# Moving the copies of a rarely entered overflow loop to VectorE, and a wait out of its If, in a hybrid decoder layer

## What is computed

```python
def hier_moe(x2d, ...):                   # 544 rows, top-1 of 4 groups, top-2 of its 8 experts
    ...                                   # e_glob: two experts for each row; w_top: their weights
    order = jnp.argsort(e_flat)
    ...                                   # rows sorted by expert, padded to blocks of 64
    def run_block(args):
        toks, e = args
        xb = x2d[toks]
        hb = jax.nn.silu(xb @ w_g[e]) * (xb @ w_u[e])
        return hb @ w_d[e]
    ...                                   # weighted outputs added back to each row
```

## Time and profile before

| | |
|---|---|
| median of 3 runs | 1580.1 us |
| lowest and highest run | 1578.76 and 1707.49 us |
| the profiled execution, its own time | 1580.1 us |
| the profiled execution, its span from the first to the last instruction | 1578.4 us |
| busy: PE / PEld / DVE / ACT / POOL | 1362.0 / 811.7 / 390.8 / 353.0 / 87.3 us |
| mean granted TensorE clock | 0.919 |

### The profile page before, as it was taken

One profiled execution on the slowest core, in us unless ns is written; L12 is line 12 of the kernel. 1 busy time (PEld: TensorE's weight loads), 2 busy tenths in 40 slices (PEclk: granted clock), 3 DMA queues, 4 the chain that ended last, 5 costly groups with the idle time before them and its releaser, 6 DMA issues.

```text
span 1578.4 us, 22203 instructions
## 1 busy us (share of the span) xinstructions
PE 1362.0 (86%) x8780; PEld 811.7 (51%) x8780; DVE 390.8 (25%) x691; ACT 353.0 (22%) x566; POOL 87.3 (6%) x144
## 2 busy tenths in 40 slices
PE   7999988986999999887699997978988888788873
PEld 5847444464676767554578884553333333233321
DVE  2013333333444444442010012241101010101113
ACT  2122233232544544664000001110100000000000
POOL 3000000002000000200000000010111001100100
PEclk9999999997999999999799998978998898889987
DMA  6113200005999999999680116036999999999984
GB/s 217 54 56 121 80 0 0 0 0 153 327 372 343 361 370 313 386 385 368 224 308 24 54 54 221 27 147 260 428 425 426 426 426 427 425 426 426 423 369 180
DMA packets 119640, 395.94 MB, mean 251 GB/s; under 512 B 17075, under 2 KB 25284, under 8 KB 107250
## 3 DMA queue, kind: packets, MB, share of 16 engines
q1 hardware_dynamic: 109506, 380.41, 62.1%
q0 software_dynamic: 5984, 11.18, 2.0%
q10 hardware_dynamic: 4048, 2.93, 0.6%
HBM read 386.06 MB, written 16.27 MB: 255 GB/s over the span
## 4 chain that ended last, share of the span: by engine, by line
PE 73%; issue 7%; DVE 6%; DMA 5%; SPq 4%; ACT 4%; ACTq 1%; POOLq 0%; DVEq 0%
PE ps L1091 16%; PE ps L932 8%; PE ps L1114 7%; PE ps L629 7%; PE ps L755 6%; PE ps L632 4%; PE ps L935 4%; PE ps L990 3%; PE ps L766 3%; DMA arena<-in_cache_k 3%; SPq L356 2%; PE ps L788 2%; PE ps L684 2%; SPq L348 1%; PE ps L688 1%
## 5 line engine op out<-in xcount | busy, mean ns | idle before, releaser
L1091 PE MATMUL ps<-arena 128*64 128x512 f32 x512 | 260.1, 667 | 73.5 <-issue 72.0
L1092 PE MATMUL ps<-arena 128*64 128x512 f32 x512 | 260.5, 669 | 0.0
L1091 PEld LDWEIGHTS ps<-arena 128*64 128x64 f32 x512 | 75.7, 154 | 222.5 <-issue 220.3
L755 PE MATMUL ps<-ident,arena 128*128 128x128 f32 x1024 | 149.3, 292 | 25.8 <-DMA arena<-in_cache_k 20.0
L755 PEld LDWEIGHTS ps<-ident,arena 128*128 128x128 f32 x1024 | 117.8, 148 | 96.2 <-issue 67.8
L1308 ACT ACTIVATE arena<-ps 128x512 f32<-128x512 f32 x192 | 108.7, 595 | 170.2 <-PE ps L755 170.0
L629 PE MATMUL ps<-mixers,arena 128*128 128x272 f32 x512 | 121.2, 399 | 0.5 <-DVE mixers L1460 0.5
L932 PE MATMUL ps<-mixers,arena 128*128 128x272 f32 x512 | 120.1, 396 | 0.0
L629 PEld LDWEIGHTS ps<-mixers,arena 128*128 128x128 f32 x512 | 98.5, 193 | 21.2 <-DVE mixers L1460 0.6
L932 PEld LDWEIGHTS ps<-mixers,arena 128*128 128x128 f32 x512 | 98.3, 192 | 20.5 <-issue 0.4
L632 PE MATMUL ps<-arena,mixers 128*128 128x512 f32 (+1 forms) x240 | 105.4, 595 | 0.0
(11 more groups left out here) (319 smaller groups left out, 1376.3 us busy)
## 6 DMA issues: line engine op xcount, KB each, us to landing
arena<-in_cache_k SPq DMA_DIRECT2D x256, 256.0 KB, 5.1
arena<-in_cache_v SPq DMA_DIRECT2D x256, 256.0 KB, 5.0
arena<-in_w_gate_exp SPq DMA_DIRECT2D x32, 2048.0 KB, 27.8
arena<-in_w_up_exp SPq DMA_DIRECT2D x32, 2048.0 KB, 32.2
arena<-in_w_down_exp SPq DMA_DIRECT2D x22, 2048.0 KB, 23.6
mixers<-in_w_down_exp SPq DMA_DIRECT2D x10, 2048.0 KB, 23.2
arena<-in_w_in SPq DMA_DIRECT2D x7, 2048.0 KB, 8.9
arena<-in_w_in SPq DMA_DIRECT2D x8, 1024.0 KB, 8.3
```

The source lines that it names most:

```text
L755: last = turn(ps[:, TURN + j % 2, P * c:P * c + P], kring[n % 3][:, j, P * c:P * c + P], ident[:, :])
L1091: mm(ps[0:BLK, 1 + u, :], own, wgv[w][:, k, :], start=k == 0, stop=k == KD - 1)
L1092: last = mm(ps[BLK:P, 1 + u, :], own, wuv[w][:, k, :], start=k == 0, stop=k == KD - 1)
```

## The change

- SP: the wait for `down` to reach 32 moves from the first place in the body of the If to a place ahead of the reading of the count, so ahead of the whole loop.
- POOL, in the body: the multiplication of gate and up is gone, and its waits are renumbered.
- ScalarE, in the body: the eight scaled copies of turned rows, the copy of the up product and the copy of the turned hidden values are gone. The SiLU and the output copy stay.
- VectorE: gets a loop of its own over the 17 passes, between `hidden_cols(31)` and the wait for the first read of `expert_outs`, with a wait for the table and a reading of the count ahead of it. In its body it scales the turned rows in one instruction, multiplies gate and up with the up product read from PSUM, and copies the turned hidden values.
- TensorE, in the body: waits for VectorE's semaphore in place of ScalarE's and POOL's.

```diff
             sp.wait_ge(S("extra_table"), 1)
+            sp.wait_ge(S("down"), NE)
             novf = sp.value_load(tab[0:1, NOVF:NOVF + 1], min_val=0, max_val=NOVF)
             with sp.Fori(0, NOVF) as i:
                 e = sp.value_load(tab[0:1, bass.ds(i, 1)], min_val=0, max_val=NE - 1)
                 with sp.If(i < novf):
-                    sp.wait_ge(S("down"), NE)
                     sp.wait_ge(S("extra_products"), extra_stage(i, 0))
...
-                    pool.wait_ge(S("extra_act"), 5 * i + 3)
-                    pool.sem_inc(S("pool_passed"), 1)
-                    nc.gpsimd.tensor_tensor(m_s[0][0:BLK, :], m_s[0][0:BLK, :], m_s[1][0:BLK, :], ALU.mult
-                                            ).then_inc(S("extra_pool"), 1)
-                    pool.wait_ge(S("extra_act"), 5 * i + 5)
+                    pool.wait_ge(S("extra_act"), 2 * i + 2)
...
-                    pe.wait_ge(S("extra_act"), 5 * i + 1)
+                    pe.wait_ge(S("extra_dve"), 3 * i + 1)
...
-                    pe.wait_ge(S("extra_pool"), i + 1)
+                    pe.wait_ge(S("extra_dve"), 3 * i + 2)
...
-                    pe.wait_ge(S("extra_act"), 5 * i + 4)
+                    pe.wait_ge(S("extra_dve"), 3 * i + 3)
...
                 with act.If(i < novf):
-                    act.wait_ge(S("extra_products"), extra_stage(i, 1))
-                    for k in range(KD):
-                        last = fn(xgT[0][:, k, 0:BLK], ps[:, 3 + k // 4, P * (k % 4):P * (k % 4) + BLK], ACT.Copy,
-                                  scale=w2c[:, k:k + 1])
-                    last.then_inc(S("extra_act"), 1)
                     act.wait_ge(S("extra_products"), extra_stage(i, 2))
                     fn(m_s[0][0:BLK, :], ps[0:BLK, 1, :], ACT.Silu).then_inc(S("extra_act"), 1)
-                    fn(m_s[1][0:BLK, :], ps[0:BLK, 2, :], ACT.Copy).then_inc(S("extra_act"), 1)
-                    act.wait_ge(S("extra_products"), extra_stage(i, 3))
-                    fn(flat(m_h[:, 0]), ps[:, 7, 0:FJ * BLK], ACT.Copy).then_inc(S("extra_act"), 1)
...
                 hidden(n)
                 hidden_cols(n)
+            dve.wait_ge(S("extra_table"), 1)
+            novf = dve.value_load(tab[0:1, NOVF:NOVF + 1], min_val=0, max_val=NOVF)
+            with dve.Fori(0, NOVF) as i:
+                with dve.If(i < novf):
+                    dve.wait_ge(S("extra_products"), extra_stage(i, 1))
+                    got = ps[:, 3:5, :].rearrange("p b (k m) -> p (b k) m", k=4)[:, :, 0:BLK]
+                    v.tensor_tensor(xgT[0][:, :, 0:BLK], got, w2c.unsqueeze(2).to_broadcast([P, KD, BLK]), ALU.mult
+                                    ).then_inc(S("extra_dve"), 1)
+                    dve.wait_ge(S("extra_act"), 2 * i + 1)
+                    own = m_s[0][0:BLK, :]
+                    v.tensor_tensor(own, own, ps[0:BLK, 2, :], ALU.mult).then_inc(S("extra_dve"), 1)
+                    dve.wait_ge(S("extra_products"), extra_stage(i, 3))
+                    v.tensor_copy(flat(m_h[:, 0]), ps[:, 7, 0:FJ * BLK]).then_inc(S("extra_dve"), 1)
+                with dve.Else():
+                    dve.nop()
+                dve.nop()
+
             for i, r in enumerate(ROWS):
                 dve.wait_ge(S(f"y_loaded_{i}"), 16)
```

## The result

The changed kernel takes 1597.53 us in the median (1594.39 to 1600.62, four runs), the kernel before 1579.43 in the same comparison. The ratio is 1.011, with a 95% interval of 1.0088 to 1.0133: 1.1% slower, under the 2% that the forecast called hard to tell from no change, but clear of zero. The one run of 1707.49 us of the kernel before is 8% slower than its other runs and doesn't enter the ratio. The forecast was 1595.0, in a range of 1591 to 1600. The profiled execution took 1598.59 us, its span is 1596.8.

What follows compares the result with a forecast made beforehand. The prediction took the tail's chain from the last down product through SP's reads of expert_outs as what matters. Body edits 0, VectorE's loop 0 and SP's wait +14.9 us on 1580.1 gave 1595.0 us, range 1591 to 1600.

Steps and rivals of the forecast that it cites:

- The edits in the body cost nothing: Body of the If on ScalarE, POOL, VectorE, TensorE: no pass enters it, so removed and added cost are 0.
- rival D: Loop over extra blocks: the count is not zero in the measured runs; given no chance of its own.
- VectorE's loop is hidden: VectorE's new loop, 10.8 us, ends before the first read of expert_outs lands, so it adds 0.
- The cover: VectorE's wait for the first read of expert_outs, hiding its loop; at least 8.7 us remain at SP's pass.
- SP's shift: SP's first issue of the expert_outs reads moves from 1557.68 to 1572.6, +14.9 us.
- SP's wait puts the loop on the chain: SP's count read and 17 empty passes now follow the last down product: +14.9 us; chance 0.80.
- Rival A: SP's 17 passes cost more or less after the last product: 1591.8 to 1598.9 us; chance 0.12.
- Rival B: VectorE's loop becomes the bound, each pass waiting for a short transfer: 1610.4 us, with two 1642.7; chance 0.05.
- Rival C: SP's moved loop is hidden anyway at L455, under 3.9 us or behind a late scatter: 1580 us; chance 0.01.
- The own range of the forecast: Whole kernel: 1593 to 1597 us around 1595.0, from undisturbed runs 1.3 us apart.
- the wide range: Whole kernel: 1591 to 1600 us, taking in both ends of SP's other pass prices with that scatter.
- everything up to 1553 unchanged: Stretch ahead of the last product's end: the profile should show no shift there, else the prediction is wrong.

Runs made afterwards that it cites:

- the two-loop kernel: All of the change but SP's moved wait, plus a second loop of 17 empty passes behind VectorE's first; ratio to the kernel before 0.9999 to 1.0047.

## Why the prediction was right, point by point

**The edits in the body cost nothing.** Right for this input. VectorE's queue has 17 branches at its If and no instruction of the body, so the count is zero here too (rival D), and the kernel with all of the change but the wait shows no difference. What the edits do to an extra block that has rows, no run here shows.

**VectorE's loop is hidden.** Right, and its size was nearly so: 10.8 us forecast; from the count's read at 1552.6 to the last branch at 1562.6 it is 10.0, with a pass of (1562.3 - 1553.7) / 16 = 0.54 us against the 0.58 taken from ScalarE. The loop's start was taken 0.4 us too late, at the end of the last column copy; the count's read stands at the copy's start. The cover was 8.7 us of spare time at SP's pass and 17.2 at the pass taken, and 18.5 were measured. The statement that without SP's shift one loop at ScalarE's pass would still cost nothing holds too: it is the kernel with all but the wait.

**SP's wait puts the loop on the chain.** Right, and the term was well sized. From release to first issue 19.0 us was forecast (1553.6 to 1572.6) and 19.3 measured in three traces; the shift is 15.2 us against 14.9. Of the 0.3 more, 0.2 are one read of the table, 0.486 us where the other sixteen take 0.26 to 0.28; without it the passes are 1.08 apart as before, and the rest is under 0.1. The long read is no accident of one execution: it is the third pass's, 3.04 us after the last copy starts, in each of the four traces in which SP reads in its loop after the last product (0.486 to 0.496). No early loop has one as long (at most 0.333). It falls together with the transfers of the last scatter (about 1559.6 to 1560.4 in the changed kernel, the read from 1559.85 to 1560.34), but whether these, or the place in the loop, make it long was not tested.

**Rival A, passes of another price after the last product.** It had 0.12 and did not come: from release to first issue it is 0.3 us more than forecast, not 3.9 more nor 3.2 less. The price that the Trainium skill gives for a tensor_load (DMA: Bandwidth & Descriptors, latency and other measured facts), about 600 ns, isn't borne out on SP: the reads of its loop take 0.27 us in the median and 0.496 at most. Of its other reads in the kernel before, one of 128 took 0.699, with the median at 0.301.

**Rival B, a transfer waited for in each pass of VectorE's loop.** Did not come: 17 passes at 0.54 us, the next 17 of the two-loop kernel at 0.53. The page of the changed kernel counts the transfers of the queue that it calls instruction (number, MB, share), and the page of the kernel before has the same line:

```profile
q8 instruction: 71, 1.16, 0.3%
```

One of the 71 falls into the 10 us of VectorE's loop, where one per pass would be 17. The rule of the Trainium skill (Runtime: NRT & Kernel Launch, Instruction fetch mechanics), that a taken branch out of the held pages stalls, is neither borne out nor refuted; no loop of VectorE here waits for a fetch in each pass, and whether its branches leave the held pages isn't known. But the mechanism beside it, a loop that outlasts the reads, is real: with two loops VectorE's queue became the bound and 5.1 us were paid.

**Rival C.** Did not come. It wanted the loop under 3.9 us; even with half the passes, or with the read out of them, it took over 8. The last scatter took 2.6 us as before.

**What was mis-sized is the scatter.** The own range of the forecast, 1593 to 1597, was put together from two undisturbed runs that lay 1.3 us apart. The median came at 1597.5, outside it though inside the wide range, which had been widened for rival A and holds only those 1.3 us for scatter. The medians lie 18.1 us apart: 15.2 are the tail, against 14.9 forecast, and 2.9 lie ahead of the last product, where the forecast has nothing. That the total still fell into the range is in this part luck. With 23 runs of the kernel before, they reach from 1573.3 to 1588.7. The prediction's test "everything up to 1553 unchanged" was for the same reason too sharp: one profile against one other can't decide about 3 us there. That 2% is about what a measurement of this kernel can tell was the opposite mistake: the intervals of the ratios here are 0.2 to 0.3% to either side.

## What to carry to other kernels

- A wait in the body of a loop whose body is never entered costs nothing, and the same wait ahead of the loop is always executed. Count what is queued behind it: each empty pass that used to run early (here 17 x 1.09 us, with the reading of the count 19.3 us where the copy and the scatter beside them take 4.1).
- Empty passes aren't free. Put loads of registers behind the If, not ahead of it (1.09 to 0.51 us per pass), and put the whole loop under one branch on the count, which took SP's passes out of the tail altogether. Both were run only with a count of zero.
- Where executions scatter by several us, measure a change in a stretch from the event that opens it: from the last copy's start to the end of the span it was 24.8 to 25.0 us in four traces whose last copy lay up to 8.1 us apart.

## What the runs showed that was not expected

VectorE's sequencer reads the count at the moment at which its engine starts the last copy, not when the copy has ended: L1954 starts at 1552.6 and the copy at 1552.63, with 0.42 us to go. The other queues do the same in this trace: ScalarE's reads the count at 1556.8, when its last copy of 0.60 us has just started, and TensorE's at 1553.3, 3.5 us before the last product ends. So a queue begins with its loop while its engine still works on what it was handed.

ScalarE's empty pass became cheaper although nothing in the passes' path was edited: its branches at the If, in the changed kernel,

```profile
L1423 ACTq COMPARE_BRANCH  x17: 50/50/63, 1557.7 to 1564.7; - x17
```

are (1564.7 - 1557.7) / 16 = 0.44 us apart, against 0.58 before. The kernel with the moved wait alone, which has ScalarE's old body, shows 0.59 (1551.6 to 1561.0), and those with the shorter body 0.44 (1556.1 to 1563.1 with all but the wait). So on ScalarE the cheaper pass goes with the shorter skipped body, of two activations in place of twelve. That the length is the cause wasn't tested. GpSimd's body lost a multiplication, and its pass stayed at 0.44 to 0.45 us; TensorE's and SP's bodies kept their length but for a line, and their passes stayed as they were.
